# Rotary embedding of q, k and the index heads: halves swapped by transfers within SBUF, in place of products with a rotation matrix

## The reference

```python
h = rmsnorm(x, norm_g[l]);  proj = h @ w_in[l]
q, k, v, ga, iq, ik, iw, xr, gr, ma, mb = jnp.split(proj, offsets, axis=-1)
q  = apply_rope(q.reshape(B, S, 8, 128), cos_a, sin_a)     # also k
iq = apply_rope(iq.reshape(B, S, 16, 64), cos_i, sin_i)    # also ik, one head
attn = dsa_attention(q, k, v, iq, ik, iw)                  # index scores pick keys, then softmax
xr = causal_depthwise_conv(xr, ...); hr = rg_lru(xr, ...)  # gates, then a scan
x = x + (sigmoid(ma) * y_a + sigmoid(mb) * y_b) @ w_o[l]

def apply_rope(x, c, s):
    x1, x2 = jnp.split(x, 2, axis=-1)
    return jnp.concatenate([x1 * c - x2 * s, x2 * c + x1 * s], axis=-1)
```

## Time and profile before

| | |
|---|---|
| median of 3 runs | 2718.02 us (2717.69 to 2720.17) |
| the profiled execution | 2723.02 us, its span 2721.2 us |
| TensorE busy | 2559.6 us, 94% |
| VectorE busy | 1993.2 us, 73% |
| ScalarE busy | 1526.0 us, 56% |
| POOL busy | 181.3 us, 7% |
| POOL's transfers (queue q0) | 5248 packets, 10.23 MB, 1.2% of 16 engines |

### The profile page before, as it was taken

How to read it: one execution, slowest core, us unless ns; L and a number is a source line. 1 busy time by engine, 2 the same in 40 slices (tenths; PEclk the granted TensorE clock), 3 DMA queues, 4 the chain that set the end, 5 groups by cost and what they waited for, 6 DMA issues and landing times. The chain is left out here.

```text
span 2721.2 us, 47747 instructions
## 1 busy us (share of the span) xinstructions
PE 2559.6 (94%) x20277; PEld 2108.3 (77%) x20277; DVE 1993.2 (73%) x2855; ACT 1526.0 (56%) x2207; POOL 181.3 (7%) x192
## 2 busy tenths in 40 slices
PE   8999999989997999999999999998999889999888
PEld 7779987689964676767676676666969879969778
DVE  7855549555357999999898999895857865757865
ACT  5634434323124777878787787764446454446444
POOL 0000000020002800000000000100200101200101
PEclk9999999999988999999999999999989999999999
DMA  6315533400033999999999999974515534625533
GB/s 195 101 62 186 163 132 115 136 20 4 4 138 140 384 365 377 366 378 374 374 378 366 378 377 367 360 300 130 175 54 173 178 118 140 195 62 171 169 106 104
DMA packets 264614, 565.87 MB, mean 208 GB/s; under 512 B 25996, under 2 KB 204356, under 8 KB 221260
## 3 DMA queue, kind: packets, MB, share of 16 engines
q1 hardware_dynamic: 257580, 547.02, 57.1%
q0 software_dynamic: 5248, 10.23, 1.2%
q10 hardware_dynamic: 1568, 5.51, 0.6%
HBM read 545.41 MB, written 11.53 MB: 205 GB/s over the span
## 5 line engine op out<-in xcount | busy, mean ns | idle before, releaser
L319 DVE TENSOR_TENSOR wl<-raw,wh 128x1024 fp32r<-128x1024 f32 (+1 forms) x610 | 742.8, 1224 | 337.4 <-ACT wh L310 321.7
L310 ACT ACTIVATE wh<-raw 128x1024 fp32r<-128x1024 f32 (+1 forms) x610 | 639.9, 1053 | 459.6 <-PE PS L163 404.6
L319 DVE TENSOR_TENSOR wl<-early,wh 128x1024 fp32r<-128x1024 f32 x384 | 466.5, 1228 | 52.8 <-ACT wh L310 33.9
L310 ACT ACTIVATE wh<-early 128x1024 fp32r<-128x1024 f32 x384 | 405.9, 1060 | 130.9 <-PE PS L163 115.0
L161 PE MATMUL PS<-wh,xe_h 128*96 128x512 f32 x896 | 357.5, 399 | 10.6 <-DVE wl L319 8.8
L161 PE MATMUL PS<-b_hn_h,wh 128*128 128x256 f32 (+1 forms) x1152 | 339.6, 295 | 21.1 <-DVE wl L319 14.6
L162 PE MATMUL PS<-wl,xe_h 128*96 128x512 f32 x896 | 354.3, 395 | 0.0
L163 PE MATMUL PS<-wh,xe_l 128*96 128x512 f32 x896 | 354.2, 395 | 0.0
L162 PE MATMUL PS<-b_hn_l,wh 128*128 128x256 f32 (+1 forms) x1152 | 332.2, 288 | 0.0
L163 PE MATMUL PS<-b_hn_h,wl 128*128 128x256 f32 (+1 forms) x1152 | 331.9, 288 | 0.0
L161 PEld LDWEIGHTS PS<-b_hn_h,wh 128*128 128x128 f32 (+1 forms) x1152 | 225.7, 196 | 27.5 <-DVE wl L319 16.9
(11 more groups left out here) (495 smaller groups left out, 4952.3 us busy)
## 6 DMA issues: line engine op xcount, KB each, us to landing
early<-in_moe_in SPq DMA_DIRECT2D x128, 1024.0 KB, 6.8
raw<-in_moe_in SPq DMA_DIRECT2D x96, 1024.0 KB, 6.7
raw<-in_w_in SPq DMA_DIRECT2D x76, 1024.0 KB, 5.4
early<-in_moe_out SPq DMA_DIRECT2D x64, 1024.0 KB, 5.9
raw<-in_moe_out SPq DMA_DIRECT2D x48, 1024.0 KB, 5.2
raw<-in_attn_w_in SPq DMA_DIRECT2D x24, 512.0 KB, 5.2
raw<-in_rw_w_rkv SPq DMA_DIRECT2D x12, 1024.0 KB, 5.1
raw<-in_ffn_w_gate SPq DMA_DIRECT2D x11, 1024.0 KB, 5.3
```

The costliest lines, as they stand in the source:

```text
L310: act.e.activation(st.two(n)[0], st.raw(n), ACT.Copy).then_inc(*act.sig("hi", st.name, n, sem=f"hi_{st.name}"))
L319: dve.e.tensor_tensor(lo, st.raw(n), hi.bitcast(F32), SUB).then_inc(*dve.sig("lo", st.name, n, sem=f"lo_{st.name}"))
```

## The change

The products on TensorE go, with their constant matrices. POOL instead copies the swapped halves of a rotation's tiles into `bt1` by transfers within SBUF: two transfers for tiles of q or k, four for iq and ik. For iq they are issued ahead of the head gathers, for ik, q and k behind them. A swap waits until its tiles are taken from PSUM and, where `bt1` was used by an earlier rotation, until that one is done. VectorE multiplies `bt1` in place by the sines; the minus sign moves into the table of sines, made by a scale per partition (columns 195 and 196 of `mcst`). `c_b2` shrinks from 768 to 512 columns, and the first use of the causal mask waits for it.

```diff
 def tables_act
-            act.e.activation(si, si, ACT.Sin)
+            act.e.activation(si, si, ACT.Sin, scale=mcst[:, 195 + i:196 + i])
 def second_pe
-        def rotate(name, x, i, f0, n=2):
-            b, before = bank("spun", l, name, f0)
-            pe.wait_ge(pe.at(*before))
-            pe.wait_ge(pe.at("ik", l) if name == "ik" else pe.at(name, (l, f0 + 1)))
-            for f in range(n):
-                t = e.matmul(PS[:, b, f * 256:(f + 1) * 256], rot[i], x[:, f0 + f, :], start=True, stop=True)
-            t.then_inc(*pe.sig("rot_mm", l, name, f0))
         def beside(p):
-            if p < 4:
-                rotate("q", q, 0, 2 * p)
-            elif p < 36:
+            if 4 <= p < 36:
                 index((p - 4) // 16, (p - 4) % 16)
-            elif p < 40:
-                rotate("k", k_, 0, 2 * (p - 36))
         for u in range(KC):
-            if 1 <= u <= 4:
-                rotate("iq", iq, 1, 2 * (u - 1))
-            if u == 5:
-                rotate("ik", ik, 1, 0, 1)
             projected(pe, l, "q", u)
 def second_dve
         def rotate(name, x, i, f0, n=2):
             co, si = cs[i]
-            b = bank_of["spun", l, name, f0]
-            src, sh = x[:, f0:f0 + n, :], [128, n, SEQ]
-            dve.wait_ge(dve.at("rot_mm", l, name, f0))
+            src, sp, sh = x[:, f0:f0 + n, :], bt1[:, f0:f0 + n, :], [128, n, SEQ]
+            dve.wait_ge(dve.at("swapped", l, name, f0))
             dve.wait_ge(dve.last)
-            e.tensor_tensor(bt1[:, f0:f0 + n, :], PS[:, b, 0:n * SEQ].rearrange("p (c t) -> p c t", c=n), bc(si, sh, 1),
-                            MUL).then_inc(*dve.sig("spun", l, name, f0))
+            e.tensor_tensor(sp, sp, bc(si, sh, 1), MUL).then_inc(*dve.sig("spun", l, name, f0))
             e.tensor_tensor(src, src, bc(co, sh, 1), MUL).then_inc(*dve.own())
             dve.wait_ge(dve.at("spun", l, name, f0))
             dve.wait_ge(dve.last)
-            e.tensor_tensor(src, src, bt1[:, f0:f0 + n, :], ADD).then_inc(*dve.sig("rot", l, name, f0))
+            e.tensor_tensor(src, src, sp, ADD).then_inc(*dve.sig("rot", l, name, f0))
 def top
+                dve.wait_ge(dve.at("c_b2"))
                 e.tensor_tensor(o, o, ca, ADD).then_inc(*dve.own())
 def second_pool
+        def swap(name, x, half, f0, n=2):
+            pool.wait_ge(pool.at("ik", l) if name == "ik" else pool.at(name, (l, f0 + 1)))
+            if name != "iq":
+                pool.wait_ge(pool.at("rot", l, "ik" if name == "q" and f0 == 0 else "q" if name == "k" else "iq", f0))
+            for p in range(0, 128, half):
+                to = p ^ half
+                e.dma_start(bt1[to:to + half, f0:f0 + n, :], x[p:p + half, f0:f0 + n, :]).then_inc(
+                    *pool.sig("swapped", l, name, f0, sem=f"swapped{f0}", by=16))
+
+        for f0 in range(0, KC, 2):
+            swap("iq", iq, 32, f0)
         for n in range(NRB):
             for p, q_, f in BY_HEAD[n]:
                 pool.wait_ge(pool.at("conv", l, f))
                 e.dma_start(CX[p, n, :], C1[q_, f, :]).then_inc(*pool.sig("heads", l, by=16))
+        swap("ik", ik, 32, 0, 1)
+        for name, x in (("q", q), ("k", k_)):
+            for f0 in range(0, KC, 2):
+                swap(name, x, 64, f0)
```

More of the change, by code:

```diff
@@ L49 @@
 NC_RW = TS + 9 * 56 + 8
-NC_B2 = 256 + 512
+NC_B2 = 512
 O_Q, O_K, O_V, O_GA, O_IQ, O_IK, O_XR, O_GR, O_MA, O_MB = 0, 1024, 2048, 3072, 4096, 5120, 5200, 6608, 8016, 9040
@@ L2324, in build @@
     bcst = tile("c_b2", NC_B2)
-    rot = [bcst[:, 0:128], bcst[:, 128:256]]
-    causal = bcst[:, 256:768].rearrange("p (a b) -> p a b", a=2)
+    causal = bcst.rearrange("p (a b) -> p a b", a=2)
     def both(name, a, b, dt=None):
@@ L3212, in constants @@
     b2 = np.zeros((128, NC_B2), f)
[L3213 to L3218, removed]
     for x in range(2):
         qp = x * 128 + np.arange(128)
-        b2[:, 256 + x * 256:512 + x * 256] = np.where(np.arange(SEQ)[None, :] <= qp[:, None], 0.0, NEG)
+        b2[:, x * 256:256 + x * 256] = np.where(np.arange(SEQ)[None, :] <= qp[:, None], 0.0, NEG)
     moe = np.zeros((128, 224), f)
@@ L3230, in constants @@
         moe[:, 193 + x] = inv[np.arange(128) % half]
+        moe[:, 195 + x] = np.where(np.arange(128) % dim < half, -1.0, 1.0)
     return {"c_moe": moe, "c_b2": b2, "c_base": base, "c_dist": dist.reshape(128, 3 * T), "c_rw": rw}
```

## The result

The changed kernel takes 2723.82 us (median of 20 runs, 2712.04 to 2732.29), the kernel before 2720.14 us on the same chip (20 runs, 2710.67 to 2729.52). The ratio is 1.002, with a 95% interval of 1.0011 to 1.0028: the change costs about 0.2% where the forecast was 0.6% faster, 2702.3 us. The measured time lies outside the range given, 2695 to 2712.

A forecast was written before the change was run, and what follows sets the result against it. TensorE was taken to set the pace, VectorE close behind; 2 x 4.1 us up to the gate products plus 3.5 and 4.0 in the gate stage made 15.7 us, from 2718.0 to 2702.3 us, range 2695 to 2712.

The forecast's parts named there:

- 13 fewer PSUM banks taken in turn: All stages: the shift in who waits for whose bank was priced at zero, between -1 and +1 us.
- 4.1 us a layer at the gate products: Gain up to the gate products: 5.6 less three charges of 0.5 us, between 0.8 and 5.6.
- I take 0.5: Before the first q rotation: VectorE's wait for the first q swap, 0.5 us taken from 0 to 2.3.
- they add nothing: Later q swaps follow at 1.06 us each while a rotation takes 2.2, so no further wait.
- the v load beside the second k swap: End of k stage: the swap shares engines with the 1 MB load, 0.5 us charged, between 0 and 1.
- 4 pairs at full-clock worth: Second sixteen gate products: removing k's four product pairs saves 3.5 us, 4.0 in the second layer with a bank wait.
- the 5.6 us at k0: 6.5 pairs of rotation products before the end of projection k0 go, 5.6 us a layer.
- rival (c): Half clock carries on into the first sixteen gate products: 2741 us at full price; chance 0.05 with any other loss.
- 0.5 for the clock: k stage: longer TensorE idle time before k6 costs 0.5 us more at half clock, between 0 and 1.5.
- (b): Swaps come late: q rotations wait up to 2.3 us, k's compete with the v load; 9.1 us gained, 2708.9; chance 0.16.
- (d): Products hidden anyway: VectorE waits 0.6 us in each of 12 rotations a layer; gain 1.3 us, 2716.7; chance 0.11.
- three signs of being wrong: VectorE waiting over 2.5 us at swaps, first v load landing after 6.5 us, or clock 0.5 in first sixteen gate products.

The follow-up runs named there:

- e1: Changed kernel with units 3 to 7 of `out` put on PSUM banks 7, 0, 1, 2, 3 instead of 5, 6, 7, 0, 1: 2715.54 us, ratio 0.9987.
- e2: Kernel before with units 3 to 7 of `out` put on the changed kernel's banks 5, 6, 7, 0, 1: 2728.36 us, ratio 1.0039.
- e4: e1 with the q halves swapped into a tile of their own (M) instead of `bt1`: 2707.76 us, ratio 0.9961.
- e5: e4 plus eight unread products on TensorE where the k rotation's products stood among the gate products: 2706.42 us, ratio 0.9946.
- e10: e8 with the k halves exchanged by products again, q, iq and ik by transfers: 2713.22 us, ratio 0.9976.
- e8: e4 with two ScalarE and VectorE splits of v weights moved into the second sixteen gate products: 2692.45 us, ratio 0.9904.
- e9: Kernel before with only the same moves of the splits as e8: 2725.97 us, ratio 1.0022.
- e6: e4 with the k halves exchanged by products again, q, iq and ik by transfers: 2707.77 us, ratio 0.9953.
- e11: e8 with the transfers of the second pair of k heads issued 10 us later: 2690.36 us, ratio 0.9893.
- e3: e1 without any of POOL's 36 swap transfers a layer, VectorE multiplying the unswapped values: 2704.08 us, ratio 0.995.

## Why the prediction was wrong

By the marks, the forecast was -15.7 us for two layers, and +4.6 came: 20.3 us apart, in three places.

- **The banks: 10.3 us.** The failed step is "13 fewer PSUM banks taken in turn ... zero, the banks -1 to +1". It named the mechanism (who waits for whose bank) and then priced it without following it. 13 is 5 modulo 8, and one look at who holds the bank that unit 3 of `out` now gets would have shown unit 1. Shown by e1 and e2.
- **The swaps of q, and with them the k stage: 2.9 us** (5.1 in e1, the same up to there, without the early k0 of after's second layer). Forecast 4.1 us a layer at the gate products; k7 came 2.9 and 2.4 sooner. "I take 0.5" for the first q swap was 2.21 us in the first layer and 1.29 in the second, inside the bounds of 0 to 2.3. But "they add nothing" failed for the second swap, which added 0.68 and 2.48: 2.9 and 3.8 us a layer in all. Gathers issued one by one had given the landing time, while these eight are let go together. The Trainium skill's figure (DMA: Bandwidth & Descriptors, Anatomy of one DMA), from which the prediction estimated 2.3 us, is what pairs of k took with no load beside them, 2.3 to 3.2, and far from the eight, 6.5. That VectorE is full from there on was right, and is why every wait was paid: e4 gives back 2.7 us in the first layer. For the v load beside the second k swap 0.5 us was given, at most 1.0; the load took 6.6 us from its issue to its use in after, from 5.5, 1.1 more, and as much more in the second layer. The two rows of after, timelines of SP and ScalarE:

```profile
1964.77 0.40 SPq L297 DMA_DIRECT2D raw<-in_w_in  x1
```

```profile
1971.38 1.06 ACT L310 ACTIVATE wh<-raw 128x1024 fp32r<-128x1024 f32 x1 [7.12 <-DMA raw<-in_w_in]
```

- **The gate stage: 7.2 us.** "What is saved is 4 pairs at full-clock worth" failed with its premise, "the clock is back at 2030, and not earlier without the pairs". It did not come back at all until the v stage: the products taken out were what brought it back (e5). The forecast thought of a clock that returns earlier or at the same time, never later. A slip of its sum is small beside this: 3.5 and the wait of 0.68 make 4.2 for the second layer, not 4.0.

What held: the 5.6 us at k0, to the tenth; POOL's issues of 0.50 to 0.52 us (medians); the iq and ik swaps hidden; the first instruction of a rotation at 692 ns as before; TensorE's idle time before k6 grown, if to 4.18 us and not to 5 or 6; the first sixteen gate products at full clock, so not rival (c). The "0.5 for the clock" in the k stage does not show: from the use of the v load to k7 after takes 1.1 us less than before in the first layer, not more. Among the rivals (b) had the right mechanism for the q swaps: its 2.3 us were less than the 2.9 and 3.8 waited, yet its 0.8 us a layer at the gate products was less than the 2.9 and 2.4 that came. (d) had the right size of gain, about none, for a wrong reason: it took new waits in all 12 rotations of a layer, and two had one. No run shows VectorE or POOL slower from the two inputs in SBUF. Of the three signs of being wrong two came: VectorE waited more than 2.5 us at swaps, and the first v load landed 6.6 us after its issue, just over the 6.5 given (6.3 in the second layer).

Put together: set the banks right, and the change gives 3.4 us by its layers (e1); give q its own scratch, and it gives 10.1 (e4), inside the range forecast; move two splits out of the gate products, and the k part, worthless till then, gives 16.7 (e10 to e8), and the whole 23.9 (e8), by the medians 20.8 and 27.7. The kernel before gains nothing from the last step (e9), so the transfers are what makes it possible. What stays open: why a layer's later stages differ by 1 to 3 us between kernels that are equal there; it goes with the granted clock of each execution, but no run here controlled that.

## What to carry to other kernels

A product taken out of a kernel takes its PSUM bank out of the turn as well: list who holds each bank after the change, in every later stage, before calling that part free. Transfers that share one scratch are let go together and here landed late together, so give them separate space or issue each as its input comes. And before counting the time of work removed beside a half-clock stretch, ask whether that work is what ends the stretch; the better remedy is to take away the idle time that started it.

## What the runs showed of the hardware

- Eight transfers of 128 KB within SBUF, issued by POOL within 4 us beside weight loads, landed in a median of 6.5 us (after) and 6.8 (e1); spread over 11 us, also beside loads, in 3.7 to 4.7 (e4, e5, e6, e8, e10, e11). Two at a time landed in 2.3 to 3.2 with no load beside them, in 3.4 to 4.6 with a load or the eight still under way (after, e4).
- A load of 1 MB, the first of v, took 6.3 to 6.9 us from issue to use with two transfers of 128 KB issued just before it (after, e1, e4, e5, e8, two layers each), and 5.2 to 5.7 without them (before, e2, e3, e6, e9, e10, e11).
- TensorE, busy without a break on gate products of 88 rows after an idle time of 2.2 us, was granted 0.50 through all twelve of them, some 10 us, and about 3 us into the v products (e4); with eight products of 128 rows among them 0.57 over 4 us and then 1.00 (e5); without the idle time it stayed at 1.00 on the same gate products (e8). That the clock follows how busy the array has lately been, as the Trainium skill says (TensorE: Matmul & The Clock Gate, The HAM clock gate), fits the fall after idle time. That it returns after sustained work, as the same section says, does not fit e4, where steady gate products did not bring it back, and here the measurement decides; in e8 they kept it.
- The first 40 us of the second layer had a granted clock of 0.96 or 1.00 with the same instructions, 1.5 us apart.
